# Score blocks of the second branch on the full array: 128x128 matmuls and masks in place of 64x64 ones

## The reference

```
def hgrn2_chunk_step(state, inp):
    q, k, g, v = inp
    b = jnp.cumsum(g, axis=2)
    causal = jnp.tril(jnp.ones((B_CHUNK, B_CHUNK), dtype=bool))
    diff = b[:, :, :, None, :] - b[:, :, None, :, :]
    decay = jnp.exp(jnp.where(causal[:, :, None], diff, -jnp.inf))
    scores = jnp.einsum('bhtd,bhsd,bhtsd->bhts', q, k, decay)
    o = (jnp.einsum('bhts,bhsv->bhtv', scores, v)
         + jnp.einsum('bhtd,bhdv->bhtv', q * jnp.exp(b), state))
    b_end = b[:, :, -1:, :]
    state = (state * jnp.exp(b_end)[:, :, 0, :, None]
             + jnp.einsum('bhsd,bhsv->bhdv', k * jnp.exp(b_end - b), v))
    return state, o
```

## Time and profile before

| | |
|---|---|
| median of 3 runs | 2331.47 us (2327.27 to 2335.48) |
| the profiled execution | 2335.48 us, of it 2334.0 us from first to last instruction |
| mean granted TensorE clock | 0.968 |
| PE busy | 2188.7 us (94%) |
| DVE busy | 1669.9 us (72%) |
| ACT busy | 1254.8 us (54%) |

### The profile page before, as it was taken

How to read it: one execution, slowest core, us unless ns; L and a number is a source line. 1 busy time by engine, 2 the same in 40 slices (tenths; PEclk the granted TensorE clock), 3 DMA queues, 4 the chain that set the end, 5 groups by cost and what they waited for, 6 DMA issues and landing times.

```text
span 2334.0 us, 44982 instructions
## 1 busy us (share of the span) xinstructions
PE 2188.7 (94%) x18911; PEld 2015.9 (86%) x18911; DVE 1669.9 (72%) x2511; ACT 1254.8 (54%) x1858; POOL 0.2 (0%) x4
## 2 busy tenths in 40 slices
PE   7789998999898999999989999999989999999998
PEld 7589898999888999889989899989977888877776
DVE  6567967788675796778877568876656445477886
ACT  5245545566554554556664356765345344466665
POOL 0000000000000000000000000000000000000000
PEclk9999999999899999989989999999989999999999
DMA  5524435477512443547754239974306555489895
GB/s 213 191 87 142 145 109 181 155 247 249 170 67 75 146 136 127 177 137 250 247 174 169 82 122 345 318 245 139 115 1 218 170 199 184 153 312 331 319 326 188
DMA packets 119355, 429.33 MB, mean 184 GB/s; under 512 B 13424, under 2 KB 16240, under 8 KB 119024
## 3 DMA queue, kind: packets, MB, share of 16 engines
q1 hardware_dynamic: 116736, 424.20, 52.9%
q10 hardware_dynamic: 2416, 2.24, 0.3%
HBM read 425.34 MB, written 1.05 MB: 183 GB/s over the span
## 4 chain that ended last, share of the span: by engine, by line
PE 81%; DVE 11%; ACT 5%; issue 2%; DMA 1%; ACTq 0%; SPq 0%; DVEq 0%
PE bank L848 80%; DVE arena L2371 4%; DVE w_low L2339 3%; ACT w_high L1789 1%; DVE arena L2380 1%; ACT arena L2069 1%; PE bank L1672 1%; DVE arena L2390 0%; PE bank L996 0%; ACT arena L2013 0%; DMA ring<-in_weights 0%; DVE arena L2375 0%; DMA ring<-in_moe 0%; DVE arena L2383 0%; ACT arena L1795 0%
## 5 line engine op out<-in xcount | busy, mean ns | idle before, releaser
L2339 DVE TENSOR_TENSOR w_low<-ring,w_high 128x1024 fp32r<-128x1024 f32 x702 | 828.9, 1219 | 92.1 <-ACT w_high L1789 91.9
L848 PE MATMUL bank<-u_high,w_high 128*128 128x256 f32 x2592 | 748.2, 289 | 30.6 <-DVE u_low L2371 24.7
L1789 ACT ACTIVATE w_high<-ring 128x1024 fp32r<-128x1024 f32 x702 | 706.2, 1052 | 92.1 <-PE bank L848 77.5
L848 PE MATMUL bank<-u_low,w_high 128*128 128x256 f32 x2592 | 740.4, 286 | 0.0
L848 PE MATMUL bank<-u_high,w_low 128*128 128x256 f32 x2592 | 739.7, 285 | 0.0
L848 PEld LDWEIGHTS bank<-u_high,w_high 128*128 128x128 f32 x2592 | 503.2, 194 | 42.5 <-issue 31.2
L848 PEld LDWEIGHTS bank<-u_low,w_high 128*128 128x128 f32 x2592 | 503.1, 194 | 0.1
L848 PEld LDWEIGHTS bank<-u_high,w_low 128*128 128x128 f32 x2592 | 502.3, 194 | 0.0
L848 PE MATMUL bank<-arena 64*64 64x64 f32 (+7 forms) x4712 | 205.7, 238 | 30.4 <-issue 10.5
L848 PEld LDWEIGHTS bank<-arena 64*64 64x64 f32 (+3 forms) x4712 | 177.7, 144 | 56.1 <-issue 32.5
L848 PE MATMUL bank<-w_high,u_high 128*128 128x256 f32 (+1 forms) x480 | 165.2, 344 | 0.0
(11 more groups left out here) (307 smaller groups left out, 3088.0 us busy)
## 6 DMA issues: line engine op xcount, KB each, us to landing
ring<-in_weights SPq DMA_DIRECT2D x539, 512.0 KB, 4.5
ring<-in_moe SPq DMA_DIRECT2D x264, 512.0 KB, 5.2
const<-in_const SPq DMA_DIRECT2D x1, 2395.0 KB, 16.1
out<-x_res ACTq DMA_DIRECT2D x2, 512.0 KB, 3.0
x_res<-in_x SPq DMA_DIRECT2D x1, 512.0 KB, 5.0
x_res<-in_x ACTq DMA_DIRECT2D x1, 512.0 KB, 5.5
const<-in_par ACTq DMA_DIRECT2D x1, 334.0 KB, 2.9
params<-in_par ACTq DMA_DIRECT2D x1, 247.0 KB, 10.2
```

Source lines behind the costliest of these rows:

```text
L848: return pe.matmul(out, lhsT, rhs, start=start, stop=stop, skip_group_check=loose)
L1789: act.activation(WH[:, ORDER.slot[cut], :], weights("s", cut), Copy).then_inc(s_hi, 1)
L2339: dve.tensor_tensor(WL[:, b, :], weights("s", cut), WH[:, b, :].bitcast(f32), SUB).then_inc(s_lo, 1)
```

## The change

Each level computes 128x128 blocks of scores: two neighbouring chunks together, with the part between the chunks set to zero by the mask. That makes 8 matmuls per level, in two banks of four each, with a mark for each bank. The masks become 128 columns wide, and the sum `sc_b` and the product `tmp8` twice as large (1024 floats per partition). VectorE masks a level with two operations, one per bank, and its add covers 1024 elements. Levels alternate between banks 0, 1 and 2, 3.

In the output `y` the score part becomes 8 matmuls over 128 tokens, and all of `y` waits for `kend`; before, its score part waited only for the sum of the scores. The third state is made in bank 4 in place of bank 3. On VectorE the copy `probT13` is moved behind level 4. The last nine side jobs use banks 7 and 5 in the other order.

```diff
-    ("level0", CH), ("level1", CH), ("level2", CH), ("level3", CH),
-    ("level4", CH), ("level5", CH), ("level6", CH), ("swap32", 128), ("swap64", 128),
+    ("level0", 128), ("level1", 128), ("level2", 128), ("level3", 128),
+    ("level4", 128), ("level5", 128), ("level6", 128), ("swap32", 128), ("swap64", 128),
...
-        put(f"level{n}", (i // (2 * h) == j // (2 * h)) & (i % (2 * h) < h) & (j % (2 * h) >= h))
-    put("level6", i == j)
+        put(f"level{n}", (r // (2 * h) == q // (2 * h)) & (r % (2 * h) < h) & (q % (2 * h) >= h))
+    put("level6", r == q)
...
-    sc_b, tmp8 = (flat(ap).rearrange("p (g c) -> p g c", c=CH) for ap in (PB[:, 4:6, :], Y[:, 4:6, :]))
+    sc_b, tmp8 = h4(flat(PB[:, 4:8, :])), h4(flat(Y[:, 4:8, :]))
...
-        j_side[layer] = jobs_of(s0 + ORDER.GATES + 6, 18, gat[:, 0:18, :], (7, 5), before=j, one="act")
+        j_side[layer] = jobs_of(s0 + ORDER.GATES + 6, 18, gat[:, 0:18, :], (5, 7), before=j, one="act")
...
-                if n > 3:
-                    pe.wait_ge(*B.dve(f"sc{n - 4}"))
-                lt, r_ = (x, x) if n < 6 else (kin, Q)
-                for m in range(4):
-                    for at in range(4):
-                        rows, cs = slice(CH * (at % 2), CH * (at % 2 + 1)), slice(CH * at, CH * (at + 1))
-                        g = 2 * m + at // 2
-                        ins = mm(psum[n % 4][rows, CH * g:CH * (g + 1)], lt[:, m, cs], r_[:, m, cs], True, True)
-                ins.then_inc(*B.pe.mark(f"sc{n}"))
+                for bk in TWO:
+                    if n > 1:
+                        pe.wait_ge(*B.dve(f"sc{n - 2}{bk}"))
+                    for j in range(4):
+                        m, cs = 2 * bk + j // 2, slice((j % 2) * P, (j % 2 + 1) * P)
+                        lt, r_ = (x, x) if n < 6 else (kin, Q)
+                        ins = mm(psum[2 * (n % 2) + bk][:, j * P:(j + 1) * P], lt[:, m, cs], r_[:, m, cs], True, True)
+                    ins.then_inc(*B.pe.mark(f"sc{n}{bk}"))
...
-                    ins = mm(psum[(4, 6, 3)[c]][:, m * P:(m + 1) * P], khat[rows, c // 2, m, :],
+                    ins = mm(psum[(4, 6)[c % 2]][:, m * P:(m + 1) * P], khat[rows, c // 2, m, :],
...
-            pe.wait_ge(*B.dve("scores"))
+            pe.wait_ge(*B.dve("kend"))
             for m in range(4):
-                for c in range(4):
-                    rows = slice(CH * (c % 2), CH * (c % 2 + 1))
-                    mm(y_chunk(c, m), VB[rows, c // 2, m * P:(m + 1) * P], sc_b[rows, 2 * m + c // 2, :],
-                       m == 0 and c < 2, c == 0, True)
-            for c in (1, 2, 3):
-                if c != 2:
-                    pe.wait_ge(*B.dve("queries" if c == 1 else "kend"))
-                for m in range(4):
-                    ins = mm(y_chunk(c, m), st_b[c][:, m * P:(m + 1) * P], Q[:, m, c * CH:(c + 1) * CH], False, True, True)
+                bank = psum[(4, 6)[m // 2]]
+                for a in TWO:
+                    at0 = (m % 2) * T + a * P
+                    mm(bank[:, at0:at0 + P], VB[:, a, m * P:(m + 1) * P], sc_b[:, 2 * m + a, :], True, False, True)
+                    for c in (2 * a, 2 * a + 1):
+                        if c:
+                            ins = mm(bank[:, at0 + (c % 2) * CH:at0 + (c % 2 + 1) * CH],
+                                     st_b[c][:, m * P:(m + 1) * P], Q[:, m, c * CH:(c + 1) * CH], False, True, True)
...
-                if n > 1:
-                    prior(d)
-                dve.wait_ge(*B.pe(f"sc{n}"))
-                tt(d, sc_b if n == 0 else tmp8, ps8(n % 4), b8(f"level{n}"), MUL, f"sc{n}")
+                for bk in TWO:
+                    dst = (sc_b if n == 0 else tmp8)[:, 4 * bk:4 * bk + 4, :]
+                    if n > 1 and bk == 0:
+                        prior(d)
+                    dve.wait_ge(*B.pe(f"sc{n}{bk}"))
+                    tt(d, dst, ps4(2 * (n % 2) + bk), b4(f"level{n}"), MUL, f"sc{n}{bk}")
...
             fill(side, FILL_B[3], last)
+            level(4)
             probs_turned(1, 3)
-            level(4)
             fill(side, FILL_B[4], last)
...
-            tt(d, h4(st_b[3]), h4(st_b[3]), ps4(3), ADD, "kend")
+            tt(d, h4(st_b[3]), h4(st_b[3]), ps4(4), ADD, "kend")
```

More of the change, by code:

```diff
@@ L343 @@
     "b_pe":
-        "sc0 sc1 sc2 sc3 sc4 sc5 turned0 turned1 s0 s1 sc6 s2 y mean roots",
+        "sc00 sc01 sc10 sc11 sc20 sc21 sc30 sc31 sc40 sc41 sc50 sc51 turned0 turned1 s0 s1 sc60 sc61 s2 y "
+        "mean roots",
     "b_act":
@@ L810, in build @@
     CONSTS = 4
-    y_chunk = lambda c, m: ps8((4, 6)[c % 2])[:, 2 * m + c // 2, :]
-    y_chunks = Y[:, 4:8, :].rearrange("p m (a h c) -> p (m a) h c", h=2, c=CH)
     after_ffn, after_mix = psum[7][:, 0:T], psum[0][:, T:2 * T]
@@ L2657, in distances @@
                 if n > 1:
-                    dve.wait_ge(*B.pe(f"sc{n - 2}"))
+                    dve.wait_ge(*B.pe(f"sc{n - 2}1"))
                 tt(d, lo, ref, b_lo, SUB)
@@ L2702, in level @@
                 if n:
-                    dve.wait_ge(*d(f"sc{n}"))
-                    tt(d, sc_b, sc_b, tmp8, ADD, "scores" if n == 6 else "-")
+                    dve.wait_ge(*d(f"sc{n}1"))
+                    tt(d, sc_b, sc_b, tmp8, ADD)
             return keys_log, keys, forget, first_level, level
@@ L2758, in branches_b_c @@
             level(6)
-            tt(d, Q, Q, eb_b, MUL, "queries")
+            tt(d, Q, Q, eb_b, MUL)
             fill(side, FILL_B[6], last)
@@ L2774, in merge @@
             for n in TWO:
-                copy(b, y_chunks[:, :, n, :], ps8((4, 6)[n]), "y" if n else "-")
+                copy(b, Y[:, 4 + 2 * n:6 + 2 * n, :], ps_t((4, 6)[n]), "y" if n else "-")
             dve.wait_ge(*G.act("high_y1"))
```

## The result

| kernel | median, us (range, runs) | ratio to before, 95% interval | profiled execution, span | mean granted clock |
|---|---|---|---|---|
| before | 2330.48 (2327.27 to 2335.48, 4) | | 2335.48, 2334.0 | 0.968 |
| with the change | 2367.93 (2366.27 to 2370.68, 4) | 1.0156 [1.0138, 1.0176] | 2361.86, 2360.4 | 0.960 |

The change costs 37.5 us by the medians, where 21.5 was predicted; it is slower, as forecast, but above the range of 2341 to 2363 us. The page answers to the earlier trace rows: TensorE is busy 18 us longer and still holds the chain.

What follows compares the result with a forecast made beforehand. VectorE's list was taken to set the pace up to `values_of(1)`, TensorE's rows behind it. Per layer 7.06 + 0.63 + 2.30 = 9.99 us, twice 19.98, plus 1.5 for the clock: 21.5, giving 2353.0 us, range 2341 to 2363.

Steps and rivals of the forecast that it cites:

- the term for the clock: Behind the longer wait ahead of `values_of(1)`: half clock in both layers, 1.5 us more in layer 1, none in layer 0; bounds 0 and 6.
- level 0 to `values_of(1)`: TensorE's start at `values_of(1)` moves 7.06 us later per layer; the copy's term in it was bounded by 0 and 9.
- VectorE's list: VectorE's work up to the copy `probT13`: masks and adds 2.09 us, copy behind level 4 4.97 us, together 7.06 per layer.
- from there to the states (level 5): Behind the copy, level 5 costs 0.63 us per layer of a TensorE without idle time.
- states to the end of `y`: `y` waits for a later `kend` and ends 2.30 us later per layer, level 6's 0.63 included; bounds 0.4 and 3.5.
- A level: Each level costs TensorE 0.63 us more; 0.54 by the skill's drain rule, with the sum falling 0.3 us.
- Side job 11: TensorE stalls 3.3 us (1.8 in layer 1) behind level 0, absorbed with the levels' cost; without that cover 10 us over both layers.
- The half-clock case: Rival: half clock behind every new wait, 1.5 us per `kend` wait and 1.7 for level 1's mask in layer 0; 2357.7 us, chance 0.16.
- Given back later: Rival: behind the branches, 7.6 us of TensorE's waits for low halves of weights come back; 2345.4 us, chance 0.12.

Runs made afterwards that it cites:

- a_warm: The changed kernel with TensorE's waits behind level 0, ahead of `probT13` and ahead of `kend` filled with identity products nobody reads; 2343.66 us, ratio 1.0048.
- a_narrow_edits_back: The changed kernel with the copy's place, the bank order and the staging of `y` taken back, leaving the wide blocks alone; 2333.29 us, ratio 1.0007.
- a_y: The changed kernel with `y` staged as before and the third state in its own bank again; 2351.03 us, ratio 1.0063.
- a_bank: The changed kernel with the old order of banks 7 and 5 for the last nine side jobs; 2360.24 us, ratio 1.0109.
- b_job_ahead: The kernel before with one TensorE side job moved ahead of its wait for `probT13`; 2319.59 us, ratio 0.9941.
- b_y_kend: The kernel before with all of `y` waiting for `kend` in place of `scores`; 2337.18 us, ratio 1.0026.
- b_copy_late: The kernel before with VectorE's copy `probT13` moved behind level 4; 2343.42 us, ratio 1.0046.

## Why the prediction was wrong

The step that failed is the term for the clock: 1.5 us in the sum, 12 to 14 us in the branches beyond what before has itself. The prediction put it so: "Behind a wait more than twice as long I expect it in both layers: 1.5 us more in layer 1, none in layer 0." The forecast left out the waits ahead of `y` and the one at side job 11. By its steps, per layer 0 and 1:

| step | predicted | the change | `a_warm`, clock 1.00 |
|---|---|---|---|
| level 0 to `values_of(1)` | 7.06 | 9.51, 8.46 | 6.76, 8.34 |
| of it VectorE's list | 7.06 | 9.23, 8.31 | 6.76, 6.76 |
| from there to the states (level 5) | 0.63 | 1.09, 2.31 | -1.14, 0.47 |
| states to the end of `y` | 2.30 | 5.54, 5.85 | 2.28, 2.30 |
| sum of both layers, without clock | 20.0 | | 19.0 |
| clock | 1.5 | 32.8 less 19.0 = 13.8 | |

- **The rows.** At full clock the three edits and the wide levels cost what was worked out, within 2 us. The -1.14 holds the 1.5 us of half clock that before itself has in layer 0 and `a_warm` lacks, and the 8.34 holds 1.7 us of lag (4.31 against 2.62); with both put right the sum is 18.8 against 20.0. So the clock of the change costs 12 us beyond before's own as the branches have it, 14 with the lag taken out, against 1.5 predicted and a bound of 6.
- **A level.** From the last side row ahead of level 0 to the second behind it TensorE takes 1.51 us in before (257.33 to 258.84) and 2.02 in `a_narrow_edits_back` (257.10 to 259.12), so level 0 costs 0.51 us more and not 0.63, nearer to the 0.54 that the prediction named beside it. That 0.54 would have taken 0.2 us off the sum, not 0.3, since level 6 stands under the wait for `kend`.
- **Where it sits.** `y`: 3.26 and 3.55 us. `values_of(1)` and what follows: 2.23 and 1.84. VectorE's list, by the masks that wait behind side job 11: 2.47 and 1.55 (42.06 and 41.14 less 39.59).
- **Side job 11.** "The wait for the copy absorbs them and they cost nothing" holds where TensorE keeps its clock (`a_warm`, and layer 1 of `a_y`), and failed in both layers of the change, where the half clock made VectorE's list 2.60 and 1.68 us longer than in `a_bank`. VectorE's masks waiting for TensorE had been written down as the upper bound of that term, 9 us; layer 0 passed it with 9.51. The 3.3 us that were read from layer 0 go with its lag of 4.22 us in that one execution: with a lag of 2.7 to 2.9 the wait is 1.7 to 2.0 us in either layer. And the price without that cover, "10 us over both layers", is 8.9 by the prediction's own numbers (5 and 6.5, less 1.3 each).
- **The rivals.** The half-clock case had the mechanism, including level 1's mask, but was given 0.16 against the forecast's 0.62, and its own 2357.7 us is too low as well; its price of 1.5 us per `y`, taken from a block of 32 rows, was less than half. `y` is longer and nothing but the clock was late there, so nearly all of its lengthening reaches the end. "Given back later" did not happen: TensorE's waits for low halves of weights between 345 and 620 us are 3.9 us, as in the earlier trace rows (3.8), and the rest of the span shows no return that can be told from scatter:

```profile
PE bank L847 <- DVE w_low L2336: 3.9, 2, 3.4
```

- **The waits for `kend`.** They are followed by half clock, with 1.53 us of wait. The Trainium skill, page TensorE: Matmul & The Clock Gate, section HAM oscillation, tells of half clock behind waits of some 3 to 5 us between bursts of matmuls. The trace agrees for the waits of 5.5 to 7.2 us ahead of `values_of(1)` (10 of 10 times), but here waits of 1.0 to 1.5 us ahead of `y` brought it 10 of 10 times too, which that section does not tell of; here the measurement decides.
- **Open.** The branches explain 32.8 us of the profiled change and the medians say 37.5; the profiled execution is 6 us faster than the median, and the rest of the span scatters by 12 us over the profiled executions, which is enough for the difference but doesn't show its cause.

## What to carry to other kernels

Price a new wait of the engine that bounds the kernel as its length plus what the rows behind it lose at half clock (here for 3 to 10 us, a whole block of 40 rows in the case of `y`), and check whether another engine waits for that block in turn. Several harmless-looking edits (a copy behind a level, one wait in place of three, a bank's order) each opened such a wait; on top of the wide blocks they cost some 35 us (1.0156 less 1.0007), the wide blocks alone 5 at most by the ratio, 6.2 in the branches. Measure from what sets the pace: counted from TensorE's level 0 the stall at side job 11 seemed free in layer 1, counted on VectorE's list it was not. Before removing a wait by a finer order, look for work that is due anyway and can stand in front of it: one moved side job gained 0.6%.

## What the runs showed of the clock

Counted over the two layers of all kernels, the granted clock was at or near half behind 10 of 10 waits of 5.5 to 7.2 us ahead of `values_of(1)`, 3 of 6 of about 2.3 us, and none of two of 0.9 us; at side job 11 behind both waits of 3.6 us and 3 of 8 of 1.7 to 2.0 us; but ahead of `y` behind 10 of 10 waits of only 1.03 to 1.53 us. Ahead of `values_of(0)`, where before, `b_job_ahead`, `b_y_kend`, `b_copy_late` and `a_bank` have nine waits of 0.97 to 1.76 us, its 16 rows are busy 1.09 us each time, as at full clock. Without a wait, or with one filled by rows or by a side job, none of the starts of `values_of(1)` or `y` had it. So the length of a wait alone does not decide; what it is about the place ahead of `y` was not tried. That rows without any use win back 25 us was not expected either (10 to 14 were); 13.8 of them are located in the branches.
